# A state-space layer's input taps, computed on VectorE instead of GpSimd beside a dense SwiGLU stage

## The reference

```python
def swiglu(h, w_gate_up, w_down):
    g, u = jnp.split(h @ w_gate_up, 2, axis=-1)
    return (jax.nn.silu(g) * u) @ w_down

def s5_layer(...):
    dt = jnp.exp(log_dt)[:, None]
    mag, ang = jnp.exp(lam_re * dt), lam_im * dt
    a_re, a_im = mag * jnp.cos(ang), mag * jnp.sin(ang)
    ...                                   # f = (a - 1) / lambda
    bb_re = f_re[..., None] * b_re - f_im[..., None] * b_im
    bb_im = f_re[..., None] * b_im + f_im[..., None] * b_re
    bu_re = jnp.einsum('blgc,gpc->lbgp', u, bb_re)
    bu_im = jnp.einsum('blgc,gpc->lbgp', u, bb_im)
    _, _, x_re, x_im = lax.associative_scan(_complex_affine_combine, (a_re_t, a_im_t, bu_re, bu_im), axis=0)
    y = einsum(x_re, c_re) - einsum(x_im, c_im)
```

## Time and profile before

| | us |
|---|---|
| median of three runs | 2009.87 (2006.34 to 2012.96) |
| the profiled execution | 2010.3 |
| its span, first to last instruction | 2008.7 |
| busy: PE / DVE / ACT / POOL | 1810.5 / 1277.1 / 997.5 / 360.8 |
| mean granted TensorE clock | 0.957 |

### The profile page before, as it was taken

One profiled execution on the slowest core, in us unless ns is written; L12 is line 12 of the kernel. 1 busy time (PEld: TensorE's weight loads), 2 busy tenths in 40 slices (PEclk: granted clock), 3 DMA queues, 4 the chain that ended last, 5 costly groups with the idle time before them and its releaser, 6 DMA issues.

```text
span 2008.7 us, 26869 instructions
## 1 busy us (share of the span) xinstructions
PE 1810.5 (90%) x10949; PEld 1646.1 (82%) x10949; DVE 1277.1 (64%) x1084; ACT 997.5 (50%) x870; POOL 360.8 (18%) x459
## 2 busy tenths in 40 slices
PE   6989297969989999999989889999988999999996
PEld 6979286857878898889878889997976888888885
DVE  4435246557456888888875544444434689888885
ACT  4454122214345666666653434333373566666663
POOL 5627988881000000000000000000011000000000
PEclk9999698979999999999999999999999899999998
DMA  8606274655437999999964216534531799999993
GB/s 285 202 31 208 75 246 150 216 198 206 151 124 252 323 318 331 318 320 325 335 222 143 88 44 219 184 130 157 191 124 43 244 319 318 331 316 328 327 326 114
DMA packets 242007, 441.09 MB, mean 220 GB/s; under 512 B 5969, under 2 KB 205681, under 8 KB 240897
## 3 DMA queue, kind: packets, MB, share of 16 engines
q1 hardware_dynamic: 235456, 414.63, 59.7%
q0 software_dynamic: 6464, 25.22, 3.8%
HBM read 426.06 MB, written 13.76 MB: 219 GB/s over the span
## 4 chain that ended last, share of the span: by engine, by line
PE 73%; POOL 12%; DVE 6%; DMA 3%; ACT 3%; issue 2%; DVEq 0%; POOLq 0%; SPq 0%; ACTq 0%
PE PS L283 20%; PE PS L285 20%; PE PS L284 20%; DVE wlo L335 3%; DMA s_tables<-t_out 3%; POOL t_out L1010 2%; POOL t_out L1011 2%; POOL t_tmp L1012 2%; PE PS L1359 2%; POOL t_out L1013 1%; POOL t_tmp L1009 1%; POOL t_out L1008 1%; PE PS L1404 1%; PE PS L1097 1%; PE PS L1369 1%
## 5 line engine op out<-in xcount | busy, mean ns | idle before, releaser
L335 DVE TENSOR_TENSOR wlo<-raw,whi 128x3072 fp32r<-128x3072 f32 (+3 forms) x279 | 866.7, 3114 | 282.1 <-ACT whi L328 280.5
L328 ACT ACTIVATE whi<-raw 128x3072 fp32r<-128x3072 f32 (+3 forms) x279 | 708.4, 2540 | 434.4 <-PE PS L285 432.6
L283 PE MATMUL PS<-wlo,hT_hi 128*128 128x384 f32 (+3 forms) x1936 | 633.1, 327 | 11.8 <-DVE hT_lo L1611 2.8
L285 PE MATMUL PS<-whi,hT_hi 128*128 128x384 f32 (+3 forms) x1936 | 626.8, 324 | 0.0
L284 PE MATMUL PS<-whi,hT_lo 128*128 128x384 f32 (+3 forms) x1936 | 626.7, 324 | 0.0
L283 PEld LDWEIGHTS PS<-wlo,hT_hi 128*128 128x128 f32 x1936 | 367.0, 190 | 23.9 <-DVE wlo L335 6.9
L284 PEld LDWEIGHTS PS<-whi,hT_lo 128*128 128x128 f32 x1936 | 367.2, 190 | 3.7 <-issue 0.7
L285 PEld LDWEIGHTS PS<-whi,hT_hi 128*128 128x128 f32 x1936 | 366.9, 190 | 0.3
L447 POOL TENSOR_TENSOR stat<-stat,cst 128x1 f32<-128x1 f32 x18 | 14.9, 833 | 813.5 <-DVE stat L424 807.4
L283 PE MATMUL PS<-wlo,mhi 128*128 128x512 f32 x352 | 143.2, 407 | 16.4 <-DVE mlo L1624 16.4
L285 PE MATMUL PS<-whi,mhi 128*128 128x512 f32 x352 | 139.2, 395 | 0.0
(11 more groups left out here) (343 smaller groups left out, 2489.7 us busy)
## 6 DMA issues: line engine op xcount, KB each, us to landing
raw<-in_moe_w_gate_up SPq DMA_DIRECT2D x96, 1536.0 KB, 7.1
raw<-in_moe_w_down SPq DMA_DIRECT2D x48, 1536.0 KB, 7.1
raw<-in_ffn_w_gate_up SPq DMA_DIRECT2D x28, 1536.0 KB, 7.1
raw<-in_moe_w_gate_up SPq DMA_DIRECT2D x32, 1024.0 KB, 6.2
raw<-in_ffn_w_down SPq DMA_DIRECT2D x14, 1536.0 KB, 6.6
raw<-in_sb_w_qkv SPq DMA_DIRECT2D x12, 1536.0 KB, 7.4
raw<-in_moe_w_down SPq DMA_DIRECT2D x16, 1024.0 KB, 6.2
raw<-s_tables SPq DMA_DIRECT2D x8, 1536.0 KB, 7.1
```

The lines of the kernel that those rows point to most:

```text
L283: pe.matmul(o, sh, mlw, start=start, stop=False, skip_group_check=True)
L285: return pe.matmul(o, sh, mh, start=False, stop=stop, skip_group_check=True)
L328: act.activation(whi[p0 % SPL][:, 0:n], raw[p0 % RAW][:, 0:n], ACT.Copy).then_inc(hi_done, 1)
L335: dve.tensor_tensor(wlo[p0 % SPL][:, 0:n], raw[p0 % RAW][:, 0:n], whi[p0 % SPL][:, 0:n].bitcast(F32), ALU.subtract).then_inc(lo_done, 1)
```

## The change

VectorE makes the taps of block j right behind the split that follows the multiply of group j (`s5_taps_dve`). They go into the buffer `g_out`, which grows from 1280 to 2304 columns beside the powers, and `t_out` shrinks from 1792 to 768. The table's columns are reordered so that the powers and the taps are adjacent: GpSimd stores `t_out` (now turns and conj(F B), 384 KB), waits for VectorE's taps, stores `g_out` (1152 KB), and then issues the loads of the next block. `s5_gd`, which the powers signalled, is now signalled by the taps.

```diff
-                   ("g_out", [P, 4, 2, 5, 32], F32), ("g_tmp", [P, 4, 4, 32], F32), ...
+                   ("g_out", [P, 2304], F32), ("g_tmp", [P, 512], F32), ...
-                   ... ("t_out", [P, 1792], F32),
+                   ... ("t_out", [P, 768], F32),
@@ dense_dve, behind the split that follows the multiply
                     split_lo(dve, p + SPL)
+                    if f == 0:
+                        s5_taps_dve(dve, j)
@@
-        T_G, T_B, T_W, T_R = slice(0, 1280), slice(1280, 1536), slice(1536, 2560), slice(2560, 3072)
+        T_G, T_W, T_B, T_R = slice(0, 1280), slice(1280, 2304), slice(2304, 2560), slice(2560, 3072)
@@ s5_tables_pool, block c
-                pool.wait_ge(s5_afr, 64 * (c + 1))
-                bt = nat[:, 0:256].rearrange("p (q a s) -> p q a s", q=2, a=1)
-                b0, b1 = (bt[:, q].to_broadcast([P, 4, P]) for q in range(2))
-                tw = tmp[:].rearrange("p (n s) -> p n s", n=4)
-                product(o_w[:, :, 0], o_w[:, :, 1], af[:, :, 0], af[:, :, 1], b0, b1, tw, ALU.add, ALU.subtract)
-                pool.dma_start(tabs[c, :, 1280:3072], out[:]).then_inc(s5_tw, 16)
+                pool.dma_start(tabs[c, :, 2304:3072], out[:]).then_inc(s5_tw, 16)
+                pool.wait_ge(s5_gd, c + 1)
+                pool.dma_start(tabs[c, :, 0:2304], ff["g_out"][:]).then_inc(s5_gw, 16)
                 if c + 1 < KC:
                     load(c + 1)
-                pool.wait_ge(s5_gd, c + 1)
-                pool.dma_start(tabs[c, :, T_G], ...).then_inc(s5_gw, 16)
@@ behind block 7
             pool.wait_ge(s5_tw, 16 * KC)
+            pool.wait_ge(s5_gw, 16 * KC)
             ...
-            pool.wait_ge(s5_gw, 16 * KC)
@@ s5_taps_dve, new
+            dve.wait_ge(s5_nat, 16 * (c + 2))
+            dve.wait_ge(s5_afr, 64 * (c + 1))
+            dve.tensor_tensor(o[:, :, 0], af[:, :, 0], b0, ALU.mult)
+            link(dve.tensor_tensor(tmp, af[:, :, 1], b1, ALU.mult))
+            dve.tensor_tensor(o[:, :, 1], af[:, :, 1], b0, ALU.mult)
+            link(dve.tensor_tensor(o[:, :, 0], o[:, :, 0], tmp, ALU.add))
+            link(dve.tensor_tensor(tmp, af[:, :, 0], b1, ALU.mult))
+            dve.tensor_tensor(o[:, :, 1], o[:, :, 1], tmp, ALU.subtract).then_inc(s5_gd, 1)
```

More of the change, by code:

```diff
@@ L221, in hybrid_trunk @@
                    ("alo0", [P, 3 * L], F32R), ("alo1", [P, 3 * L], F32R),
-                   ("g_out", [P, 4, 2, 5, 32], F32), ("g_tmp", [P, 4, 4, 32], F32), ("g_nat", [P, KC, 4, 2, 32], F32),
-                   ("t_af", [P, 4, 2, P], F32), ("t_nat", [P, 512], F32), ("t_out", [P, 1792], F32),
+                   ("g_out", [P, 2304], F32), ("g_tmp", [P, 512], F32), ("g_nat", [P, KC, 4, 2, 32], F32),
+                   ("t_af", [P, 4, 2, P], F32), ("t_nat", [P, 512], F32), ("t_out", [P, 768], F32),
                    ("t_tmp", [P, 512], F32), ("t_pow", [P, ST, 2, 4], F32),
@@ L1019, in s5_tables_pool @@
                 o_b = out[:, 0:256].rearrange("p (r q o) -> p r q o", r=4, q=2)
-                o_w = out[:, 256:1280].rearrange("p (n q s) -> p n q s", n=4, q=2)
-                o_r = out[:, 1280:1792].rearrange("p (a r v u) -> p a r v u", a=2, r=4, v=8)
+                o_r = out[:, 256:768].rearrange("p (a r v u) -> p a r v u", a=2, r=4, v=8)
                 shape = [P, 4, 8, 8]
@@ L1060, in link @@
                 dve.wait_ge(chain_v, k[0])
-            o, tmp, pa, cn_ = ff["g_out"], ff["g_tmp"], ff["t_pow"], ff["g_nat"]
+            o, pa, cn_ = ff["g_out"][:, T_G].rearrange("p (r q i o) -> p r q i o", r=4, q=2, i=5), ff["t_pow"], ff["g_nat"]
+            tmp = ff["g_tmp"][:].rearrange("p (r i o) -> p r i o", r=4, i=4)
             if c == 0:
@@ L1073, in s5_powers_dve, with s5_taps_dve, link @@
             dve.tensor_tensor(o[:, :, 0, 1:5, :], cr, pr, ALU.mult)
-            link(dve.tensor_tensor(tmp[:], ci, pi, ALU.mult))
+            link(dve.tensor_tensor(tmp, ci, pi, ALU.mult))
             dve.tensor_tensor(o[:, :, 1, 1:5, :], cr, pi, ALU.mult)
-            link(dve.tensor_tensor(o[:, :, 0, 1:5, :], o[:, :, 0, 1:5, :], tmp[:], ALU.subtract))
-            link(dve.tensor_tensor(tmp[:], ci, pr, ALU.mult))
-            dve.tensor_tensor(o[:, :, 1, 1:5, :], o[:, :, 1, 1:5, :], tmp[:], ALU.add).then_inc(s5_gd, 1)
+            link(dve.tensor_tensor(o[:, :, 0, 1:5, :], o[:, :, 0, 1:5, :], tmp, ALU.subtract))
+            link(dve.tensor_tensor(tmp, ci, pr, ALU.mult))
+            link(dve.tensor_tensor(o[:, :, 1, 1:5, :], o[:, :, 1, 1:5, :], tmp, ALU.add))
+            CHAIN_V[0] = k[0]
+        def s5_taps_dve(dve, c):
+            k = [CHAIN_V[0]]
+            def link(ins):
+                k[0] += 1
+                ins.then_inc(chain_v, 1)
+                dve.wait_ge(chain_v, k[0])
+            o = ff["g_out"][:, T_W].rearrange("p (n q s) -> p n q s", n=4, q=2)
+            tmp, af = ff["g_tmp"][:].rearrange("p (n s) -> p n s", n=4), ff["t_af"]
+            bt = ff["t_nat"][:, 0:256].rearrange("p (q a s) -> p q a s", q=2, a=1)
+            b0, b1 = (bt[:, q].to_broadcast([P, 4, P]) for q in range(2))
+            dve.wait_ge(s5_nat, 16 * (c + 2))
[6 more added lines that the diff above has]
+            dve.tensor_tensor(o[:, :, 1], o[:, :, 1], tmp, ALU.subtract).then_inc(s5_gd, 1)
             CHAIN_V[0] = k[0]
```

1 line of the change is left out of this document (removed).

## The result

The changed kernel takes 1949.28 us (median of four runs, 1948.57 to 1950.73), the kernel before on the same chips 2010.71 (four runs, 2006.34 to 2012.96). The ratio is 0.9698, with a 95% interval of 0.968 to 0.9716: 61 us less. Forecast were 1964, with a range of 1952 to 1986. The sign was right, and so was what held the kernel before. The forecast gain was 15 us too small, since in the new kernel TensorE is the bound and not the ring that the forecast was built on; the time lies 2.7 us under the range. The profiled execution took 1948.9 us, its span is 1947.3, its mean granted clock 0.967.

A forecast was written before the change was run, and what follows sets the result against it. GpSimd's late store was taken to hold VectorE and, through it, TensorE. With multiply 1 at 238.7, rounds of 26.2 us and 20.1 at the end, `h` moves from 461.9 to 416, 45.9 us off 2010.3: 1964 us, range 1952 to 1986.

The forecast's parts named there:

- the ring: First dense stage, per group: multiply, split, taps, store of `g_out`, powers, split, multiply again; priced 26.2 us against TensorE's 25.73.
- What bounds the kernel before: First dense stage: TensorE is held by VectorE, and VectorE (120.8 us of waits) by a store that GpSimd issues late.
- The front: Start of the stage: taps and loads leave GpSimd's path, so the multiply of group 1 moves from 246.14 to 238.7.
- One round of the new chain: Groups after multiply 1: terms from multiply to multiply sum to 26.2 us, including landing 7.6 and powers 6.4.
- Taps: VectorE's six 512-element operations per block: 4.1 us a round, the first ones free in 4.47 us of idle time.
- The end of the stage: From multiply 7 at 395.9 to the norm's `h` at 416, where `h` was at 461.9: 45.9 us less.
- the floor rival: Dense stage: with stores landing in 6.5 us or less TensorE's 25.73 binds; `h` near 407, 1955 us; chance 0.22.
- Late stores: Rival on stores issued while VectorE splits: landing 10.8 us, ring 29.4, total 1986 us; chance 0.26.
- the rule against the change: VectorE and GpSimd exclude one another for whole operations: taken to the end, ring 31.1 us and time about 1993.
- The order's worth: Front of the stage: storing `g_out` ahead of the five loads instead of behind them, 2.5 us.
- The columns' new order: Table columns read behind the stage: the reordering was claimed to cost nothing.

The follow-up runs named there:

- the first early variant: Against the changed kernel: GpSimd stores `g_out` 0 amid its preparations, `g_out` 1 at their end, later ones ahead of their own turns; 1947.55 us, ratio 0.970.

## Why the prediction was right, and where it was wrong

**What bounds the kernel before.** Right. GpSimd's table work and the store behind it held VectorE and through it TensorE; taking the taps away from GpSimd was worth 41 to 43 us, the order of the store 16 to 20.

**The front.** Right in kind, 2.5 us too long. The front landing was priced at 6.8 us and took 6.8 (222.28 to 229.07). The preparations were held up by about 2 us (turns at 215.16, 216.9 by the start of before, against 214.80), priced 3, and the powers beside the turns took 5.4 (229.07 to 234.48), priced 6.9.

**One round of the new chain: the step that failed.** Here lies half of the error. The prediction had VectorE's ring at 26.2 us per round, over TensorE's 25.73, so that the ring set the pace. In the trace a round takes 23.7 and 24.6 us at first (to multiplies 2 and 3) and 24.6 to 25.7 afterwards, where VectorE also waits 0.4 to 1.9 us for a piece that comes behind TensorE; TensorE at 25.72 sets the pace and waits for none of these multiplies. The term that was mis-sized is the powers, priced 6.4 us: in the first two rounds they took 4.8 (249.99 to 254.79) and 4.5 (274.83 to 279.30), later 5.5 to 6.2. Landing was priced 7.6 and measured 5.4 to 8.4, median 7.1. By its terms the first round was 0.87 + 3.27 + 4.37 + 7.00 + 4.80 + 3.36 = 23.67: the powers are 1.6 of the 2.5 us, the landing 0.6. I had them meet conj(F B) each time. In GpSimd's rows of these two rounds the turns are over before the powers begin, conj(F B) first waits for `t_nat`, and its 128-element operations hold VectorE up little:

```profile
249.46 0.74 POOL L1015 TENSOR_TENSOR t_out<-t_out,t_tmp 128x256 f32<-128x256 f32 x1
252.06 0.47 POOL L1010 TENSOR_TENSOR t_out<-s_par,t_nat 128x128 f32<-128x128 f32 x1 [1.87 <-DMA t_nat<-in_s_bc]
```

With 26.2 against TensorE's 25.73 a term that is 1.6 us too large decides which of the two binds. The experiments bracket it: with 2.5 us more ahead of the store the ring is at 27.3 and binds, with 3.4 us less of VectorE's work nothing is gained. What the prediction had right is TensorE's first group behind the wait, 29.9 us by before and 29.3 here (234.48 to 263.81), 3.6 over the others.

**Taps.** Right: 4.1 to 4.3 us a round (262.29 to 266.35, 188.89 to 193.15), and those of block 0 cost nothing, in the idle time that was seen there (4.47 us before, 0.18 left).

**The end of the stage.** The stretch from multiply 7 to `h` was priced at 20.1 us and took 20.4 (380.30 to 400.72). But I let multiply 7 come a full round of 26.2 us behind multiply 6, and it came after 21.9. In the group ahead of the last both splits are of pieces of 1024 elements, 1.23 and 1.36 us instead of 3.35 and 3.5, and TensorE's work is shorter too (22.72). That is 4.3 us. The trace of before has short pieces at the same places (splits at 411.61 and 439.58), and I did not read them. At the very end ring and TensorE nearly tie: VectorE is free for the last split at 380.71 and waits 0.27 us for ScalarE's half, which begins right behind TensorE's up 7.

**The sum of the errors** at multiply 7 (395.9 forecast, 382.0 with the start taken out): 2.5 at the front, 7.1 in groups 2 to 6 (131.0 forecast between multiplies 1 and 6, 123.9 measured), 4.3 in the last round. 13.9 us, and the earlier start of the stage adds 1.7, of which the `h` gives 0.3 back: 15.3 us at `h`, 416.0 for 400.72. That the time lies only 2.7 us under the range is partly the floor rival's doing, which had pulled the range down to 1952.

**The floor rival** (chance 0.22) is what happened, from multiply 1 on, though with landings of 7.1 us at the median, over the 6.5 that it named as its condition: the shorter powers made room. Its `x` was 395.0 and came at 395.4 (393.73 + 1.7), in part by luck: it started 2.5 us too late, and TensorE waited 2.7 us for the last multiply, which it had left out. Its `h` near 407 was 4.6 us late beside 402.4, since it let the tables end some 6 us behind and they ended 1.5 behind (7.0 us from `x` to `h` for 5.5 before).

**Late stores, and the rule against the change.** Both fell. A store is issued in 0.54 us beside a split, and lands in 5.4 to 8.4 us while splits run. As for the copy from SBUF to SBUF that shuts GpSimd's descriptors out, which the Trainium skill names in "SBUF", the box on VectorE blocking DMA: no run here shows a delay that would be its. For the exclusion itself, which the Trainium skill has in "SBUF", Who interferes with whom, the trace agrees: 2.96 us for a 256-element operation of GpSimd beside a split and 0.64 alone (232.97), in the first early variant. What kept it from costing 6.9 us a round is where the turns lie, mostly in VectorE's wait for the store.

**The order's worth** was the largest single misjudgment, though it hid in the total: 2.5 us at the front, by the prediction, and 16 to 20 us by two experiments. The mechanism that the prediction lacked is the landing of `t_out`: with the loads behind the second store instead of the first it landed in 4.0 us, and the chain was GpSimd waiting for it.

**The columns' new order** costs at most 0.7 us: from one norm's `h` to the next it was 120.9 us (400.72 to 521.60), before 121.8 (461.90 to 583.69), and before has one of the 1.6 us stretches in it. The 0.7 lie ahead of the first `mm`, 9.9 us behind `h` for 9.2.

## What to carry to other kernels

When a sum of terms comes within 2% of another engine's floor, as 26.2 did of 25.73, either can be the bound: price both to the end, and let the range take in both. The last, shorter round of a loop has to be priced by its own rows. A wait at a store tells when the transfer ended, not what it costs: cutting 3.4 us ahead of a store gained nothing here, where TensorE was the bound in between and the store then landed 3.6 and 3.8 us slower at the two places looked at, and moving a store ahead of five small loads gained 16 to 20 us. Before moving a store or a wait to an earlier point, ask what the engine that issues it must still do before the next one: if it is busy all the way, the wait only changes its place. And before two profiles are compared to within a few microseconds, compare the spacing of their equal passes: a single stretch at the lower clock is 1.6 us.

## What the runs showed of the hardware

- The same store takes very different times: `t_out` of 896 KB 4.0 to 5.1 us, and 4.5 to 9.2 in another order of the same instructions; `g_out` of 1152 KB 4.4 to 6.1, 5.4 to 8.4, and 6.1 to 11.5, by what it met.
- VectorE's powers took 4.5 to 6.2 us beside GpSimd's small operations, 4.4 with few of them, while GpSimd's operations took up to nine times their time beside VectorE's long ones (0.64 to 2.96, 0.40 to 3.51 us). Who has the short operations pays.
- TensorE comes back from a long wait at the lower clock. Behind the wait of 28.4 us its granted clock was 0.50 in 225 to 236 us, 0.64 in 236 to 242 and 1.00 from 242 on; with a wait in every group, before, it was 0.84 to 0.93 in 290 to 440 us.
- The granted clock also fell to 0.50 for some 3 us with TensorE busy and no gap in the 29 us before, in one or two passes of some profiles and in none of others; each time it cost 1.6 us.

In GpSimd's rows after, one operation of conj(F B) beside the split that begins at 254.79:

```profile
254.98 3.51 POOL L1014 TENSOR_TENSOR t_tmp<-s_par,t_nat 128x128 f32<-128x128 f32 x1
```
